# First expert table: GpSimd makes half of each low part from a copy that ScalarE takes out of PSUM, and the residual rests in DRAM meanwhile

## The chip, the cores and the metric

One core of one Trainium2 chip runs the whole program. The metric is the device time of one execution in microseconds (us). The kernel before took 3082.72 us, the median of 3 runs (3081.7 to 3082.83).

## What is computed

The program is a layer of a language model on 512 tokens of width 1024, followed by two more blocks (attention, gated linear attention, feed-forward). The change lies in the first layer's mixture of experts, which has 16384 experts of one row each in two tables, `u_tab` and `v_tab`:

```python
def block_fn(xb):
    T = xb.shape[0]
    q = (xb @ wq).reshape(T, PEER_HEADS, 2, PEER_KHALF)
    s = jnp.einsum('thpc,hpnc->thpn', q, keys)
    v1, i1 = lax.top_k(s[:, :, 0], PEER_TOPK)
    v2, i2 = lax.top_k(s[:, :, 1], PEER_TOPK)
    ...
    sc, pos = lax.top_k(cand, PEER_TOPK)
    idx = jnp.take_along_axis(cidx, pos, axis=-1)
    gate = jax.nn.softmax(sc, axis=-1)
    ug = jnp.take(u_tab, idx, axis=0)
    act = jax.nn.gelu(jnp.einsum('td,thkd->thk', xb, ug), approximate=False)
    vg = jnp.take(v_tab, idx, axis=0)
    return jnp.einsum('thk,thkd->td', gate * act, vg)
```

There are 8 heads with 16 chosen experts each, so 128 experts per token. The result is added to the residual `x`. All of it is float32.

## The kernel before, in words

**Stages.** `peer_scores` (from about 450 us) makes the queries and their scores against the keys. `first_choice_and_memory` chooses the experts of the first 128 tokens. `experts_first` (about 600 to 1302 us) goes through the first table, `experts_second` (to about 1840 us) through the second. Between these functions all engines meet at the end of a block. In `peer_scores` SyncE loads the key tiles (L2163) and query weights (L250) in turn; in `experts_second` GpSimd gathers rows of v (L3147) as it gathered rows of u, and SyncE begins the loads of the next stage's weights (L448) when the last tile has been used.

**float32 in three passes.** A float32 factor is split into a high part, which TensorE multiplies at full rate, and a low part, the exact value minus the high one. A product is then three matmuls: high by high, low by high, high by low (`three_passes`, L207 to L209).

**`experts_first` (L2721).** The table has 128 tiles of 128 experts. The first 128 tokens are done exactly by gathering the rows they chose; the other 384 are multiplied with every expert, and the unwanted results get a gate of zero later. For each tile b:

- SyncE loads 128 raw rows of u, 512 KB, into one of two buffers (L2644).
- TensorE turns them (eight transposes of 128x128, L3012) into two PSUM banks, `ps_u[0]` and `ps_u[1]`, four transposes each. It is three tiles ahead: it turns tile b+3 before it multiplies tile b. Half n of a turn waits until VectorE has read that bank.
- ScalarE copies both banks as the high half (L2940, two instructions of 128x512). VectorE makes the low half (`make_low`, L2846): PSUM minus high, two instructions of 128x512. The high and low parts lie in four slots.
- TensorE multiplies: 24 matmuls of 384 columns. ScalarE applies Gelu (L2950) and stores the result (L2952).
- GpSimd gathers, for the routed tokens, one row of u per token (an indirect DMA, `fetch`, L2823) into one of four row buffers, and VectorE takes the dot product of each row with its token (L2851). `fetch(b+1)` waits until `dot(b-3)` has freed its buffer. `take_list` (L2815) gives it the next four columns of the list of experts.

**What else runs in the stage.** For each of the three remaining groups of 128 tokens there is a choice phase of 24 tiles and a gate phase of 16 tiles. In the choice phase VectorE runs the top-16 search in 24 chunks, one between every two tiles (`topk.numbers`, with lines such as L2315, L2320, L2375, L2378). In the gate phase it builds float16 marks of the chosen experts (`build`, L2896 to L2900), TensorE sums them into gates (`sum_gates`, L3034), ScalarE takes these out of PSUM (L2961) and stores 1 MB for every 32 tokens (L2965). Between the two phases TensorE waits for VectorE's signal `chosen` and turns the chosen numbers and gates (L3047). Eight tiles remain at the end. A tile takes 5.04 us in the choice phase and 5.98 us in the gate phase.

**The order of the work.** Each engine's queue is in order and written out by hand; semaphores join them. VectorE's order for tile b is: a chunk of the choice (or `build`), both halves of `make_low(b+3)`, then `dot(b)`. ScalarE's is the high part of tile b+3, the Gelu of tile b, the gates. GpSimd's is `fetch(b+1)`, and a `take_list` before every fourth.

**The residual.** `c.x` holds x, 2 MB in SBUF, from the start of the layer until `experts_second` adds the experts' result to it at its end (L3247).

Of the kernel before, what the change touches and what calls it, by code (L numbers as in the profile page):

```python
# [2125 lines left out]
WQ_SLOTS = 4  # L2126


def peer_scores(nc, c, weights, late, keys_t, scores, topk, ahead):

# [7 lines left out]
    with ExitStack() as ctx:  # L2140
# [12 lines left out]
        with nc.Block() as block:  # L2153
            @block.sync
            def _(sp):
                ahead.load(sp)
                for j in range(tiles):
                    t = j + 2
                    if slots <= t < tiles:
                        weights.load(sp, t // slots, t % slots)  # L2160
                    if j >= slots:
                        sp.wait_ge(scored, j - slots + 1)
                    sp.dma_start(keys[:, j % slots, :], keys_t[j, :, :]).then_inc(loaded[j % slots], 16)  # L2163
                sp.wait_ge(weights.low_made, tiles + 2)
                ahead.load_first_keys(sp)

            @block.gpsimd
            def _(pool):
# [475 lines left out]
        sp.dma_start(self.raw[:, b % 2, :], self.tiles[bass.ds(i * BODY + b, 1), :, :].rearrange("a p d -> (a p) d")).then_inc(self.loaded[b % 2], 16)  # L2644


class SecondTable:


# [65 lines left out]
def experts_first(nc, c, u, table, act_d, g_d, topk, h_n, dots, second):  # L2715
# [18 lines left out]
    with ExitStack() as ctx:  # L2734
# [5 lines left out]

        halves = c.h[:, :, :].rearrange("p (r a) n -> p r (a n)", r=4)
        raw, loaded = table.raw, table.loaded
        high = [x[:, :, :] for x in second.high] + [c.h_high[:, :, 0:P]]
        low = [x[:, :, :] for x in second.low] + [c.h_low[:, :, 0:P]]
        rows = [topk.scores[:, 0, n * 8:(n + 1) * 8, :].rearrange("p a k -> p (a k)") for n in range(2)]
# [18 lines left out]
        u_turned = sem("u_turned")  # L2764
        high_made = sem("high_made")
        low_made = sem("low_made")
        used = sem("used")
        act_kept = sem("act_kept")
        act_stored = second.act_stored
# [17 lines left out]
        with nc.Block() as block:  # L2787
# [23 lines left out]

            @block.gpsimd
            def _(pool):
                def take_list(i, b):
                    nc.gpsimd.tensor_copy(list_[:, b % 8:b % 8 + 4], topk.idx[:, bass.ds(i * BODY + b, 4)]).then_inc(listed, 1)  # L2815
                    pool.wait_ge(listed, i * 2 + b // 4 + 1)
                    pool.sem_inc(list_seen, 1)

                def fetch(i, b):

                    pool.wait_ge(dotted, i * BODY + b + 1)
                    pool.sem_inc(row_seen, 1)
                    nc.gpsimd.indirect_dma_start(rows[b % 4], None, u,  # L2823
                                                 bass.IndirectOffsetOnAxis(ap=list_[:, b % 8:b % 8 + 1], axis=0)).then_inc(fetched[b % 4], 16)

                def tiles(i, last):
                    for b in range(BODY):
                        if b + 1 < BODY or not last:
                            if b % 4 == 3:
                                take_list(i, b + 1)  # L2830
                            fetch(i, b + 1)

                pool.iota(line_i[:, :], pattern=[[1, KEYS]], base=0, channel_multiplier=0).then_inc(line_made, 1)
                take_list(0, 0)
                fetch(0, 0)
                with pool.Fori(0, KEYS // BODY - 1) as i:
                    tiles(i, False)
                tiles(KEYS // BODY - 1, True)

            @block.vector  # L2840
            def _(dve):
                def make_low(i, b):
                    for n in range(2):
                        dve.wait_ge(high_made, i * (2 * BODY) + 2 * b + n + 1)
                        ks = slice(4 * n, 4 * n + 4)
                        nc.vector.tensor_tensor(low[b % SLOTS][:, ks, :].bitcast(F32R), ps_u[n][:, :, :], high[b % SLOTS][:, ks, :],  # L2846
                                                ALU.subtract).then_inc(low_made, 1)

                def dot(i, b):
                    dve.wait_ge(fetched[b % 4], (i * (BODY // 4) + b // 4) * 16 + 16)  # L2850
# [83 lines left out]
            def _(act):  # L2934
                def make_high(i, b):

                    act.wait_ge(used, i * BODY + b + 1)
                    for n in range(2):
                        act.wait_ge(u_turned, i * (2 * BODY) + 2 * b + n + 1 + 4)
                        nc.scalar.activation(high[b % SLOTS][:, 4 * n:4 * n + 4, :].bitcast(F32R), ps_u[n][:, :, :], ACT.Copy).then_inc(high_made, 1)  # L2940

                def tile(i, b):
                    make_high(i, b + ahead)
                    keep(i, b)
# [23 lines left out]
                act.sem_inc(act_kept, 2)  # L2968
                act.sem_inc(gates_kept, 2)
                act.sem_inc(used, SLOTS)  # L2970
                for n in range(2):
                    act.sem_inc(act_stored[n], 16)
                    act.sem_inc(gates_stored[n], 16)
# [29 lines left out]
            def _(pe):  # L3003
# [3 lines left out]

                def turn_from(rows_in, i, b):
                    for n in range(2):
                        pe.wait_ge(low_made, i * (2 * BODY) + 2 * b + n + 1)  # L3010
                        for k in range(4 * n, 4 * n + 4):
                            mm = nc.tensor.transpose(ps_u[n][:, k - 4 * n, :], rows_in[:, k * P:(k + 1) * P], c.ident[:, :])  # L3012
                        mm.then_inc(u_turned, 1)
# [3 lines left out]
                    products(i, b)  # L3017

                def products(i, b):
                    pe.wait_ge(low_made, i * (2 * BODY) + 2 * b + 2 + 2)  # L3020
                    pe.wait_ge(act_kept, i * BODY + b + 1)
                    for k in range(DT):
                        mm = three_passes(nc, ps[b % 2][:, 0:DENSE], high[b % SLOTS][:, k, :], low[b % SLOTS][:, k, :],
                                          c.h_high[:, k, P:S], c.h_low[:, k, P:S], start=(k == 0), stop=(k == DT - 1))
                    mm.then_inc(used, 1)
# [8 lines left out]
                            mm = nc.tensor.matmul(ps_g[n % 2][:, m, :], second_hot[:, slot, t, :], first[:, slot, j, t, :], start=(j == 0), stop=(j == 1))  # L3034
                    mm.then_inc(grouped, 1)

                pe.sem_inc(low_made, 2)
                for b in range(ahead):
                    pe.wait_ge(table.head_loaded[b], 16)
                    turn_from(table.head[b], 0, b)  # L3040
# [16 lines left out]
                    products(0, b)  # L3057


def experts_second(nc, c, v, act_d, second, idx, dots, gate, following, first):  # L3060

# [4 lines left out]
    with ExitStack() as ctx:  # L3068
# [33 lines left out]
        with nc.Block() as block:  # L3102
            @block.sync
            def _(sp):
                def load(i, b, last):
                    sp.wait_ge(low_made, i * (2 * BODY) + b + 1)
                    second.load(sp, i, b)
                    if last and b >= 2 * BODY - 2:
                        sp.wait_ge(second.act_stored[b % 2], (KEYS // 2) * 16 + 16)

                    sp.wait_ge(made, i * (2 * BODY) + b + 1)
                    second.load_act(sp, act_d, i, b)

                def turn(i, first, last):
                    for b in range(2 * BODY):
                        if not first or b >= 4:
                            load(i, b, last)
                        if b % oct_ == 3 and not (last and b > oct_):

                            r = b // oct_  # L3120
                            if r == 0:
                                second.load_gates(sp, i, 1)
                            else:
                                second.load_gates(sp, i + 1, 0)

                sp.sem_inc(low_made, 4)
                sp.sem_inc(made, 4)
                turn(0, True, False)
                with sp.Fori(1, KEYS // (2 * BODY) - 1) as i:
                    turn(i, False, False)  # L3130
                turn(KEYS // (2 * BODY) - 1, False, True)
                sp.wait_ge(made, KEYS + 4)
                for b in range(first):
                    following.load(sp, b)
# [57 lines left out]
            def _(dve):  # L3192
# [49 lines left out]
                turn(KEYS // per - 1, True)  # L3242
                dve.wait_ge(row_summed, KEYS + 4)
                nc.vector.tensor_tensor(row_sum[:, 0, :], row_sum[:, 0, :], row_sum[:, 1, :], ALU.add).then_inc(rows_added, 1)
                for k in range(DT):
                    dve.wait_ge(row_turned, k + 1)
                    nc.vector.tensor_tensor(c.x[:, k, :], acc[k][:, :], c.x[:, k, :], ALU.add).then_inc(added, 1)  # L3247
# [1369 lines left out]
def experts(nc, c, a, late, weights, lasting):  # L4617
# [3 lines left out]
    with ExitStack() as ctx:  # L4621
# [6 lines left out]
        dots = sb("dots", [P, HEADS * TOPK])  # L4628
        scores = sb("scores", [P, ST, 2 * HEADS, KEYS])
        second = SecondTable(nc, c, a["v"], g_d, scores)  # L4630
        with nc.sbuf_tensor("norm2_unit_high", [P, DT, S], F32, align_bytes=ALIGN) as c.h_high, \
                nc.sbuf_tensor("norm2_unit_low", [P, DT, S], F32, align_bytes=ALIGN) as c.h_low:
            with ExitStack() as inner:
                topk = TopK(nc, c, inner, scores, idx, gate)
                memory = MemoryAhead(nc, c, a)
                peer_scores(nc, c, weights, late, a["keys_t"], scores, topk, memory)
                late.room.close()
                table = FirstTable(nc, c, a["u"])
                first_choice_and_memory(nc, c, a, topk, h_n, table, memory)
                second.share(ctx, lasting)  # L4640
                experts_first(nc, c, a["u"], table, act_d, g_d, topk, h_n, dots, second)
        retire_semaphores(c)
        stream = qkv_stream(nc, c, a)
        half = DT // 2
        stream.early = {b: tuple(x[0][:, b * half:(b + 1) * half, :].rearrange("p k n -> p (k n)") for x in (second.high, second.low)) for b in range(2)}
        experts_second(nc, c, a["v"], act_d, second, idx, dots, gate[:, 0, :], stream, 4)
    return stream


# [396 lines left out]
```

## Time and profile before

| what | value |
|---|---|
| median of 3 runs | 3082.72 us (3081.7 to 3082.83) |
| profiled execution, its span | 3083.4 us |
| TensorE (PE) busy, share of the span | 3001.1 us, 97% |
| VectorE (DVE) busy | 2225.1 us, 72% |
| GpSimd (POOL) busy | 1124.6 us, 36% |
| ScalarE (ACT) busy | 981.6 us, 32% |
| DMA | 507.91 MB, mean 165 GB/s |

The span is the time between the first and the last event of one profiled execution; the runs were timed apart from it. Of the profiled execution only the span is listed, so the span serves as its own time; it is 0.7 us over the runs' median. A busy share is an average over stages that are limited by different things, so it doesn't tell what a change in one stage is worth.

### The profile page before, as it was taken

Reading aid. Unit: us, or ns where it says so; the run is one execution under the profiler, and the core shown is the slowest. Engines: PE = TensorE matmul, PEld = TensorE weight load, DVE = VectorE, ACT = ScalarE, POOL = GpSimd, SP = SyncE. Lnnn points to the kernel's source line nnn. Section 1 sums busy time; section 2 is a strip of 40 time slices with the busy share of each in tenths; the row PEclk is TensorE's granted clock in tenths of the full one; section 3 lists DMA queues with packets and bytes.
Section 4 is the critical chain, followed back from the end, with each engine's and each line's share of the span. In section 5 each row is a group of like instructions: output and inputs, shape, how many; then the busy total and the mean of one; then the engine's idle time right before and its main releaser. Section 6 shows DMA issues by size and latency. Waiting matters only on the chain. (4 is left out here: it accounts for less than half of the span.)

```text
span 3083.4 us, 55647 instructions
## 1 busy us (share of the span) xinstructions
PE 3001.1 (97%) x20151; PEld 2650.7 (86%) x20151; DVE 2225.1 (72%) x3952; ACT 981.6 (32%) x1828; POOL 1124.6 (36%) x806
## 2 busy tenths in 40 slices
PE   9999989899999999999999999999999999899999
PEld 7688868799999999999999997768888878688887
DVE  8766687798898898688888887677775345577741
ACT  3444430334433334333333333561111023321110
POOL 4234235222122222243333334214555443345553
PEclk9999999999999999999999999999999999899999
DMA  4000032377877878899999953112223241123233
GB/s 171 28 3 3 3 113 78 131 241 254 299 247 263 286 251 268 297 388 359 352 348 340 354 202 105 33 55 89 96 99 92 79 99 35 58 88 99 98 92 93
DMA packets 242033, 507.91 MB, mean 165 GB/s; under 512 B 44566, under 2 KB 135846, under 8 KB 238412
## 3 DMA queue, kind: packets, MB, share of 16 engines
q1 hardware_dynamic: 183116, 321.11, 31.0%
q0 software_dynamic: 36864, 134.23, 13.4%
q10 hardware_dynamic: 21888, 50.34, 4.2%
q8 instruction: 106, 1.74, 0.2%
q14 instruction: 59, 0.48, 0.0%
HBM read 453.17 MB, written 52.44 MB: 164 GB/s over the span
## 5 line engine op out<-in xcount | busy, mean ns | idle before, releaser
L202 POOL TENSOR_TENSOR up_low<-normed,up_high 128x1024 fp32r<-128x1024 f32 (+1 forms) x136 | 317.0, 2331 | 299.9 <-DVE up_high L197 299.9
L3147 POOL DMA_INDIRECT ev_rows<-in_v,ev_list x128 | 177.3, 1385 | 326.5 <-DVE ev_row_sum L3214 313.6
L207 PE MATMUL up_ps<-ffn_high,up_high 128*128 128x512 f32 x704 | 274.9, 390 | 3.0 <-DVEq L833 3.0
L209 PE MATMUL up_ps<-ffn_high,up_low 128*128 128x512 f32 x704 | 273.9, 389 | 0.0
L208 PE MATMUL up_ps<-ffn_low,up_high 128*128 128x512 f32 x704 | 273.9, 389 | 0.0
L207 PE MATMUL eu_ps<-norm_unit_high,expert_high 128*128 128x384 f32 x768 | 265.7, 346 | 0.0
L209 PE MATMUL eu_ps<-norm_unit_high,expert_low 128*128 128x384 f32 x768 | 258.2, 336 | 0.0
L208 PE MATMUL eu_ps<-norm_unit_low,expert_high 128*128 128x384 f32 x768 | 257.9, 336 | 0.0
L197 DVE CAST up_high<-normed 128x1024 fp32r<-128x1024 f32 (+1 forms) x136 | 92.5, 680 | 205.4 <-PE up_down_ps L209 150.6
L2823 POOL DMA_INDIRECT expert_scores<-in_u,eu_list x64 | 84.0, 1313 | 268.3 <-DVE eu_dots L2851 260.0
L3172 ACT ACTIVATE expert_high<-mixed 128x1024 fp32r<-128x1024 f32 x95 | 100.8, 1061 | 229.3 <-PE ev_acc L209 212.9
L2846 DVE TENSOR_TENSOR expert_low<-eu_turned,expert_high 128x512 fp32r<-128x512 f32 x192 | 123.8, 686 | 66.2 <-ACT expert_high L2940 65.2
L207 PE MATMUL ev_acc<-ev_w_high,expert_high 128*128 128x384 f32 x512 | 171.1, 334 | 0.0
L209 PE MATMUL ev_acc<-ev_w_high,expert_low 128*128 128x384 f32 x512 | 171.0, 334 | 0.0
L208 PE MATMUL ev_acc<-ev_w_low,expert_high 128*128 128x384 f32 x512 | 171.0, 334 | 0.0
L2950 ACT ACTIVATE mixed<-eu_ps 128x384 f32<-128x384 f32 x128 | 62.8, 491 | 329.4 <-PE eu_ps L209 329.4
L3214 DVE SCALAR_TENSOR_TENSOR ev_row_sum<-ev_rows,ev_weight,ev_row_sum 128x1024 f32<-128x1024 f32 x128 | 164.3, 1285 | 3.4 <-DMA ev_rows<-in_v,ev_list 3.4
L791 ACT ACTIVATE mixed<-up_ps,columns_sb 128x512 f32<-128x512 f32 x88 | 68.6, 779 | 297.2 <-DVE up_ps L821 297.2
L2823 POOL DMA_INDIRECT normed<-in_u,eu_list x64 | 68.7, 1073 | 256.5 <-DVE eu_dots L2851 255.8
L3207 DVE TENSOR_TENSOR expert_low<-mixed,expert_high 128x1024 fp32r<-128x1024 f32 x95 | 117.9, 1241 | 60.4 <-ACT expert_high L3172 60.4
L207 PEld LDWEIGHTS up_ps<-ffn_high,up_high 128*128 128x128 f32 x704 | 132.1, 188 | 31.5 <-DVEq L833 3.8
L208 PEld LDWEIGHTS up_ps<-ffn_low,up_high 128*128 128x128 f32 x704 | 132.1, 188 | 27.7 <-issue 0.5
(721 smaller groups left out, 8633.5 us busy)
## 6 DMA issues: line engine op xcount, KB each, us to landing
mixed<-in_v SPq DMA_DIRECT2D x128, 512.0 KB
normed<-in_u SPq DMA_DIRECT2D x125, 512.0 KB
normed<-in_w_up SPq DMA_DIRECT2D x88, 512.0 KB, 3.4
expert_act<-mixed ACTq DMA_DIRECT2D x128, 192.0 KB
expert_gates<-eu_gates ACTq DMA_DIRECT2D x24, 1024.0 KB
expert_scores<-expert_gates SPq DMA_DIRECT2D x16, 1536.0 KB
normed<-expert_act SPq DMA_DIRECT2D x128, 192.0 KB
normed<-in_w_down SPq DMA_DIRECT2D x32, 448.0 KB, 3.3
```

Source lines behind the costliest of these rows:

```text
L197: return nc.vector.tensor_copy(high.bitcast(F32R), of)
L202: return nc.gpsimd.tensor_tensor(low.bitcast(F32R), of, high, ALU.subtract)
L207: nc.tensor.matmul(out, w_high.bitcast(F32R), x_high.bitcast(F32R), start=start, stop=False)
L208: nc.tensor.matmul(out, w_high.bitcast(F32R), x_low.bitcast(F32R), start=False, stop=False)
L209: return nc.tensor.matmul(out, w_low.bitcast(F32R), x_high.bitcast(F32R), start=False, stop=stop)
L791: nc.scalar.activation(cv[:, s, :], ps[s][:, :], ACT.Identity, scale=c.cols[:, bass.ds(j + at + 2 * 2 * FT, 1)], bias=c.cols[:, bass.ds(j ...
L2823: nc.gpsimd.indirect_dma_start(rows[b % 4], None, u, bass.IndirectOffsetOnAxis(ap=list_[:, b % 8:b % 8 + 1], axis=0)).then_inc(fetched[b % ...
L2846: nc.vector.tensor_tensor(low[b % SLOTS][:, ks, :].bitcast(F32R), ps_u[n][:, :, :], high[b % SLOTS][:, ks, :], ALU.subtract).then_inc(low_ ...
L3147: nc.gpsimd.indirect_dma_start(rows[:, b % 4, :], None, v, bass.IndirectOffsetOnAxis(ap=list_[:, b % 8:b % 8 + 1], axis=0)).then_inc(fetch ...
L3172: nc.scalar.activation(high[b % SLOTS][:, :, :].bitcast(F32R), raw[:, b % 4, :, :], ACT.Copy).then_inc(high_made, 1)
L3207: nc.vector.tensor_tensor(low[b % SLOTS][:, :, :].bitcast(F32R), raw[:, b % 4, :, :], high[b % SLOTS][:, :, :], ALU.subtract).then_inc(low ...
L3214: nc.vector.scalar_tensor_tensor(out=row_sum[:, b % 2, :], in0=rows[:, b % 4, :], scalar=weight[:, bass.ds(i * per + b, 1)], in1=row_sum[: ...
```

## The change

In `experts_first`, VectorE makes only the first half of each tile's low part. For the second half ScalarE copies bank `ps_u[1]` a second time, as it is, into one of two SBUF buffers (`copied`, the first two 128x512 pieces of `c.x`), and GpSimd subtracts the high part from that copy. TensorE's second half turn now waits for ScalarE's copy instead of VectorE's second half, and its products wait for both low halves. ScalarE's copy of tile b waits until GpSimd has read the copy of tile b-2 (`copy_low_made`). In GpSimd's loop the new `make_low(b+3)` stands ahead of `fetch(b+1)`, and the first three low parts stand ahead of the `iota`, the first list and the first fetch.

Since `c.x` is used as a buffer, the residual is stored to DRAM by SyncE in `peer_scores`, and loaded back by SyncE at the end of `experts_second`, where VectorE waits for it before its last addition. The program also clears its semaphores once more ahead of `experts_first`: `TopK` and `FirstTable` are created before `peer_scores` with their semaphores kept apart, and GpSimd clears the retired ones at the start of the block.

```diff
 def peer_scores(...):
                 ahead.load(sp)
+                residual.store(sp)
                 for j in range(tiles):
...
                 ahead.load_first_keys(sp)
+                sp.wait_ge(residual.stored, 16)
...
+class ResidualAway:
+    def __init__(self, nc, c):
+        self.x, self.away = c.x, nc.dram_tensor("residual_away", [P, DT, S], F32).ap()
...
+    def store(self, sp):
+        sp.dma_start(self.away, self.x[:, :, :]).then_inc(self.stored, 16)
+    def load(self, sp):
+        sp.dma_start(self.x[:, :, :], self.away).then_inc(self.loaded, 16)
...
 def experts_first(...):
+        copied = c.x[:, 0:2, :]
...
             @block.gpsimd
             def _(pool):
+                clear_stale(nc, c)
...
+                def make_low(i, b):
+                    pool.wait_ge(copy_made, i * BODY + b + 1 + 1)
+                    pool.sem_inc(copy_met, 1)
+                    take_low(nc, low[b % SLOTS][:, 4:8, :], copied[:, b % 2, :].rearrange("p (k n) -> p k n", n=P), high[b % SLOTS][:, 4:8, :]).then_inc(copy_low_made, 1)
+
                 def tiles(i, last):
                     for b in range(BODY):
+                        if b + ahead < BODY or not last:
+                            make_low(i, b + ahead)
                         if b + 1 < BODY or not last:
                             if b % 4 == 3:
                                 take_list(i, b + 1)
                             fetch(i, b + 1)
 
+                for b in range(ahead):
+                    make_low(0, b)
                 pool.iota(...)
...
             @block.vector
             def _(dve):
                 def make_low(i, b):
-                    for n in range(2):
-                        dve.wait_ge(high_made, i * (2 * BODY) + 2 * b + n + 1)
-                        ks = slice(4 * n, 4 * n + 4)
-                        nc.vector.tensor_tensor(low[b % SLOTS][:, ks, :].bitcast(F32R), ps_u[n][:, :, :], high[b % SLOTS][:, ks, :],
-                                                ALU.subtract).then_inc(low_made, 1)
+                    dve.wait_ge(high_made, i * (2 * BODY) + 2 * b + 1)
+                    nc.vector.tensor_tensor(low[b % SLOTS][:, 0:4, :].bitcast(F32R), ps_u[0][:, :, :], high[b % SLOTS][:, 0:4, :],
+                                            ALU.subtract).then_inc(low_made, 1)
...
             def _(act):
...
+                    act.wait_ge(copy_low_made, i * BODY + b + 1)
+                    nc.scalar.activation(copied[:, b % 2, :].rearrange("p (k n) -> p k n", n=P), ps_u[1][:, :, :], ACT.Copy).then_inc(copy_made, 1)
...
             def _(pe):
...
-                        pe.wait_ge(low_made, i * (2 * BODY) + 2 * b + n + 1)
+                        pe.wait_ge(copy_made if n else low_made, i * BODY + b + 1)
...
                 def products(i, b):
-                    pe.wait_ge(low_made, i * (2 * BODY) + 2 * b + 2 + 2)
+                    pe.wait_ge(low_made, i * BODY + b + 1 + 1)
+                    pe.wait_ge(copy_low_made, i * BODY + b + 1 + 2)
                     pe.wait_ge(act_kept, i * BODY + b + 1)
...
 def experts_second(...):
                 turn(KEYS // (2 * BODY) - 1, False, True)
+                residual.load(sp)
                 sp.wait_ge(made, KEYS + 4)
...
+                dve.wait_ge(residual.loaded, 16)
                 for k in range(DT):
                     dve.wait_ge(row_turned, k + 1)
                     nc.vector.tensor_tensor(c.x[:, k, :], acc[k][:, :], c.x[:, k, :], ALU.add).then_inc(added, 1)
...
             with ExitStack() as inner:
+                taken, c.taken = c.taken, []
                 topk = TopK(nc, c, inner, scores, idx, gate)
+                table = FirstTable(nc, c, a["u"])
+                c.apart, c.taken = c.taken, taken
...
-                table = FirstTable(nc, c, a["u"])
                 first_choice_and_memory(nc, c, a, topk, h_n, table, memory)
                 second.share(ctx, lasting)
+                retire_semaphores(c)
                 experts_first(...)
```

## Rows read from the trace of the kernel before

A row of windows gives the busy time and, in brackets, the instructions of PE, PEld, DVE, ACT and POOL in this order. Rows of a timeline give start and length in us.

**Rows 1.** Windows: stretch, length, busy us (count) by engine, clock, DMA share, GB/s.

```profile
843.00:957.00 114.00, 113.16 (x733) 112.16 (x731) 101.99 (x270) 39.35 (x74) 28.76 (x28) 1.00 0.74 245
957.00:1053.00 96.00, 96.00 (x761) 93.61 (x760) 79.06 (x145) 41.45 (x81) 21.49 (x21) 1.00 0.86 289
600.00:1302.00 702.00, 697.12 (x4870) 684.64 (x4868) 587.84 (x1363) 267.97 (x498) 160.99 (x159) 0.99 0.79 266
```

**Rows 2.** Waits of PE, 610 to 1300 us: total us, times, longest us.

```profile
PE eu_g L3034 <- DVE eu_first L2900: 2.5, 3, 0.9
```

**Rows 3.** Timeline, 683 to 692 us: start, length, engine, line, operation, count, [idle before].

```profile
685.13 1.03 PE L3012 MATMUL eu_turned<-ident,normed 128*128 128x128 f32 x8
...
686.40 0.10 DVE L2320 MATCH_VALUE_LOAD topk_pos<-topk_top,mixed 128x8 f32 x1
...
686.53 1.09 ACT L2940 ACTIVATE expert_high<-eu_turned 128x512 fp32r<-128x512 f32 x2 [0.62 <-PE eu_turned L3012]
...
689.56 1.28 DVE L2846 TENSOR_TENSOR expert_low<-eu_turned,expert_high 128x512 fp32r<-128x512 f32 x2
...
690.31 1.25 PE L3012 MATMUL eu_turned<-ident,normed 128*128 128x128 f32 x8
```

**Rows 4.** Lines by form, GpSimd: busy us, mean ns, idle us before.

```profile
L202 POOL TENSOR_TENSOR norm_unit_low<-normed,norm_unit_high 128x512 fp32r<-128x512 f32 x8 | 10.3, 1287 | 9.5 <-DVE norm_unit_high L197 9.5
```

**Rows 5.** Timeline of GpSimd and VectorE, 2143 to 2149 us.

```profile
2144.50 2.39 POOL L202 TENSOR_TENSOR up_low<-normed,up_high 128x1024 fp32r<-128x1024 f32 x1 [2.60 <-DVE up_high L197]
...
2144.84 2.60 DVE L809 TENSOR_TENSOR mixed<-mixed 128x512 f32<-128x512 f32 x1
...
2147.58 0.43 DVE L197 CAST ff_high<-mixed 128x512 f32 x1
...
2148.61 1.30 POOL L202 TENSOR_TENSOR ff_low<-mixed,ff_high 128x512 f32 x1 [1.72 <-DVE ff_high L197]
```

**Rows 6.** Timeline of GpSimd, 596 to 616 us.

```profile
601.52 0.94 POOL L2823 DMA_INDIRECT expert_scores<-in_u,eu_list  x1 [0.30 <-issue]
```

**Rows 7.** Timeline of VectorE and GpSimd, 700 to 712 us.

```profile
710.93 2.29 DVE L2375 TENSOR_TENSOR mixed<-topk_part_f,topk_ranks 128x2048 f32<-128x2048 f32 x1
...
711.82 2.21 POOL L2823 DMA_INDIRECT normed<-in_u,eu_list  x1 [3.73 <-DVE eu_dots L2851]
```

**Rows 8.** Source L3147, the second table's gathers: issue to landing.

```profile
DMA to landing us min/median/max: 4.5/7.5/10.0
```

**Rows 9.** Timeline, 957 to 970 us, the gate phase.

```profile
962.12 1.04 PE L3012 MATMUL eu_turned<-ident,normed 128*128 128x128 f32 x8
...
963.32 1.29 DVE L2900 TENSOR_TENSOR eu_first<-eu_marks,eu_part 128x1024 f16<-128x1024 f16 x2
...
964.24 1.09 ACT L2940 ACTIVATE expert_high<-eu_turned 128x512 fp32r<-128x512 f32 x2 [0.62 <-ACT eu_gates L2961]
...
967.19 1.07 PE L3034 MATMUL eu_g<-eu_first,eu_second 128*128 128x128 f16 x16
...
968.10 1.04 PE L3012 MATMUL eu_turned<-ident,normed 128*128 128x128 f32 x8
```

**Rows 10.** Timeline of PE, 724 to 746 us.

```profile
730.87 0.38 PE L3047 MATMUL eu_sel_ps<-ident,topk_number 128*128 128x128 f32 x2
```

**Rows 11.** Source L127, the clearing of semaphores: ns min, median, max.

```profile
L127 POOLq EVENT_SEMAPHORE_RANGE_CLEAR  x12: 46/157/640, 390.1 to 2643.6; - x12
```

**Rows 12.** Windows 460 to 464 us; timeline of SyncE's queue, 455 to 475 us.

```profile
460.00:462.00 2.00, 2.00 (x10) 1.61 (x10) 0.54 (x1) 1.32 (x2) 1.90 (x1) 1.00 0.90 342
462.00:464.00 2.00, 2.00 (x11) 1.65 (x10) 1.90 (x4) 0.00 (x0) 0.51 (x1) 1.00 0.19 50
...
471.83 0.33 SPq L2163 DMA_DIRECT2D wq_keys<-in_keys_t  x1
```

**Rows 13.** Timeline of SyncE's queue and VectorE, 1800 to 1834 us.

```profile
1819.56 1.75 SPq L448 DMA_DIRECT2D normed<-in_w_qk  x4
...
1833.48 0.69 DVE L3247 TENSOR_TENSOR residual<-ev_acc,residual 128x512 f32<-128x512 f32 x1 [3.41 <-PE ev_acc L3260]
```

More of the change, by code:

```diff
@@ L2126, with peer_scores @@
 WQ_SLOTS = 4
-def peer_scores(nc, c, weights, late, keys_t, scores, topk, ahead):
+def peer_scores(nc, c, weights, late, keys_t, scores, topk, ahead, residual):
     slots = WQ_SLOTS
@@ L2644, in load @@
         sp.dma_start(self.raw[:, b % 2, :], self.tiles[bass.ds(i * BODY + b, 1), :, :].rearrange("a p d -> (a p) d")).then_inc(self.loaded[b % 2], 16)
+class ResidualAway:
+    def __init__(self, nc, c):
+        self.x, self.away = c.x, nc.dram_tensor("residual_away", [P, DT, S], F32).ap()
+        self.stored, self.loaded = nc.alloc_semaphore(name="residual_stored"), nc.alloc_semaphore(name="residual_loaded")
+    def store(self, sp):
+        sp.dma_start(self.away, self.x[:, :, :]).then_inc(self.stored, 16)
+    def load(self, sp):
+        sp.dma_start(self.x[:, :, :], self.away).then_inc(self.loaded, 16)
 class SecondTable:
@@ L2766, in experts_first @@
         low_made = sem("low_made")
+        copy_made = sem("copy_made")
+        copy_low_made = sem("copy_low_made")
+        copy_met = sem("copy_met")
         used = sem("used")
@@ L2970, in _ @@
                 act.sem_inc(used, SLOTS)
+                act.sem_inc(copy_low_made, 2)
                 for n in range(2):
@@ L3035, in sum_gates @@
                     mm.then_inc(grouped, 1)
-                pe.sem_inc(low_made, 2)
+                pe.sem_inc(low_made, 1)
+                pe.sem_inc(copy_made, 1)
                 for b in range(ahead):
@@ L3057, in _, with experts_second @@
                     products(0, b)
-def experts_second(nc, c, v, act_d, second, idx, dots, gate, following, first):
+def experts_second(nc, c, v, act_d, second, idx, dots, gate, following, first, residual):
     ahead = SLOTS - 1
@@ L4630, in experts @@
         second = SecondTable(nc, c, a["v"], g_d, scores)
+        residual = ResidualAway(nc, c)
         with nc.sbuf_tensor("norm2_unit_high", [P, DT, S], F32, align_bytes=ALIGN) as c.h_high, \
@@ L4633, in experts @@
             with ExitStack() as inner:
+                taken, c.taken = c.taken, []
                 topk = TopK(nc, c, inner, scores, idx, gate)
+                table = FirstTable(nc, c, a["u"])
+                c.apart, c.taken = c.taken, taken
                 memory = MemoryAhead(nc, c, a)
-                peer_scores(nc, c, weights, late, a["keys_t"], scores, topk, memory)
+                peer_scores(nc, c, weights, late, a["keys_t"], scores, topk, memory, residual)
                 late.room.close()
-                table = FirstTable(nc, c, a["u"])
                 first_choice_and_memory(nc, c, a, topk, h_n, table, memory)
                 second.share(ctx, lasting)
+                retire_semaphores(c)
                 experts_first(nc, c, a["u"], table, act_d, g_d, topk, h_n, dots, second)
@@ L4645, in experts @@
         stream.early = {b: tuple(x[0][:, b * half:(b + 1) * half, :].rearrange("p k n -> p (k n)") for x in (second.high, second.low)) for b in range(2)}
-        experts_second(nc, c, a["v"], act_d, second, idx, dots, gate[:, 0, :], stream, 4)
+        experts_second(nc, c, a["v"], act_d, second, idx, dots, gate[:, 0, :], stream, 4, residual)
     return stream
```

## The prediction, written before the changed kernel was run

> **What bounds the kernel now.** I first cut the span into stretches to see which engine fills the one that the change is in. From 600 to 1302 us (the first expert table) TensorE is busy 697.1 of 702 us at a granted clock of 0.99; in the stretch beside the choice of experts 113.2 of 114 us, in the one with the gates 96.0 of 96.0 [rows 1]. VectorE has 102.0 of 114 us, so it is nearly full too, ScalarE and GpSimd are not. Then I asked what TensorE waits for: from 610 us on, three waits of 0.8 us each, for the first marks of each gate phase [rows 2]. So VectorE's subtraction is beside a full TensorE: all that TensorE idles here is 702 - 697.1 = 4.9 us, and that is the most that any relief can give in this stage, 0.16% of the kernel. The timeline of a tile [rows 3] shows the one place where VectorE is late with the low part: after eight searches (686.40 to 689.56) its subtraction ends half a tile at 690.16, and the next turn starts at 690.31, 0.14 us after the 5.04 us that a tile takes. About 0.4 us in all; it happens in the first table alone.
>
> **The change, part by part.** Measured chances: about 0.2% (6 us) is what can be told from no change.
>
> 1. Engines' sums. VectorE loses one 0.69 us subtraction per tile (two in 1.28, a pitch of 0.60 [rows 3]): 128 x 0.60 = 77 us. ScalarE gains one copy at its pitch, 1.09 - 0.60 = 0.49 [rows 3]: 63 us on 268. GpSimd gains 128 subtractions of 1.29 us [rows 4] = 165 us on 161. None of these reaches TensorE's 697, so by sums nothing changes; gain at most the 0.4 us above. ScalarE's new wait, ahead of its copy, is for GpSimd's low part of two tiles before; the Gelu and the gates stand behind it, but that part is made some 6 us earlier by the loop below: 0, and if GpSimd should fall a whole tile behind, it is the loop that shows it. TensorE's new wait before its products is for a low part made three tiles ahead: 0.
>
> 2. A wait put before the gathers. This is the term that decides. GpSimd's queue is in order. Before, it waits only for a free row buffer, four deep, and the row for tile b is asked for three tiles early. Now it does low(b+3), which waits for the copy of tile b+3, and only then fetch(b+1). So the gather of row b can't start until low(b+2) is made, and behind that gather stands VectorE's dot(b), behind that one chunk of the choice and the first half of low(b+4), and TensorE's turn(b+5) waits for that half. That closes a loop over three tiles. Its room is 3 x 5.04 = 15.12 us. Its length, counted from the start of turn(b+2): second copy ended 2.49 (685.13 to 687.62) and the new one 0.49 more, 2.98 [rows 3]; GpSimd's wake after a semaphore, 0.60 in one place [rows 5], between that and nothing: 0.3; low 1.29 [rows 4]; 0.30 to the next GpSimd instruction [rows 6]; gather G; dot 1.15 (its 1.22 overlaps); chunk C; half a low 0.60; TensorE's wake 0.15 [rows 3]. In sum 6.8 + G + C, so G + C may be 8.35.
>
> C from the code's 24 chunks a table: three of 3.16 us (eight searches or replacements, [rows 3]), two of 2.6, seven of 2.3 (2048 wide [rows 7]), the others 2.1 or less, 2.15 in the mean. G, from issue to landing, isn't printed for this table; the same gather of the second table takes 4.5 us at the least, 7.5 in the middle, 10.0 at the most [rows 8], there with DMA nearly full, here with a share of 0.74 to 0.86 [rows 1]. Ends 4.5 and 7.5; I take 6.0, half-way, because the share lies between a free and a full one.
>
> With G = 6.0, C over 2.35 stalls TensorE: three times 0.8, twice 0.27, and the five two-input 2048-wide chunks if something adds 0.65. It does: GpSimd's issue of a gather took 2.21 us instead of 0.94 beside such an operation [rows 7], 1.27 more; half of it, since it has to meet. That is 2.4 + 0.5 + 3.0 = 6 us a table. A stall lengthens the room of the next two tiles, and the heavy chunks follow each other, so I count half: 3 a table, 9 us. The Trainium skill (page SBUF — State Buffer, section Who interferes with whom) infers that a tensor_tensor with two SBUF inputs takes only the read interface that it shares with GpSimd, and so leaves the writing of descriptors free. Here the trace disagrees, by the 2.21 us; by the page the 3.0 would be gone, and this term 4.5 us instead of 9.
>
> 3. The same loop in the gate phase. Room 3 x 5.98 = 17.94 for the turn (962.12, 968.10), but the marks of tile b+1 are wanted earlier, at 2 x 5.98 + 5.07 = 17.03 (967.19) [rows 9]. Length: copy ended 3.21 + 0.49 = 3.70 [rows 9]; wake 0.3; low 1.29 plus a lock wait of 0.35 (half of one f16 operation); 0.30; gather 6.3 (its issue is 0.27 longer here); dot 1.15: 13.4. Then four f16 operations, 2.5 (two in 1.29 [rows 9]), one held by GpSimd's low for 0.65: that GpSimd's subtraction blocks a two-input operation is shown by one of 2.60 us, begun under a GpSimd subtraction of 2.39 [rows 5]; half of 1.29 is taken. 16.5 against 17.03. It holds in the mean and not where the 1 MB gate writes meet the gather: 1 us a table, 3 us.
>
> 4. Changes of phase. dot(22) of a table comes at turn(24) + 11.4 from part 2's sum (2.98 + 0.3 + 1.29 + 0.30 + 6.0, with 0.5 of waiting), then 2.3 and 0.9 for the gates, then the signal that TensorE waits for at 730.87 [rows 10]; turn(24) is three tiles before, 715.75: 715.75 + 11.4 + 1.15 + 3.2 = 731.5. 0.6 us late, three times: 2 us. Before, it was there in time.
>
> 5. The start: GpSimd now makes three low parts before its first gather, so dot(0) moves back by some 4 us, which VectorE has caught up but for 0.5 us when turn(7) wants low(6). The clear of stale semaphores costs at most 0.64 us a piece [rows 11] before the first copy exists: 0. At the end the last three gathers come together: 0 to 1 us, 0.5.
>
> 6. The residual. SP's store of 2 MB stands ahead of four key loads and two weight loads. The queues move 342 GB/s until the loads end at 462, as the DMA share's fall to 0.19 shows; 2.1 MB at that rate take 6 us, so these land at 468, and the first score ends at 471.8, where SP's next key load is let go [rows 12]. Cover 3.8 us: 0; without it, up to 6. The load back is issued after the last tile's loads, ahead of the next weight loads at 1819.56; VectorE idles 3.41 us before it adds onto the residual [rows 13], which hides a last gather that is late: 0; without that cover 3.
>
> Sum: 9 + 3 + 2 + 1 - 0.4, about +14. The profiled execution has a span of 3083.4, 0.7 over the median of 3082.7, so 3097 by its own time, 3096 as a median.
>
> **The rivals.** (a) The gather lands in time. G = 4.5: G + C stays under 8.35 in every chunk, the gate phase has 2 us of room, and only a lock here or there is left: 3083, from 3079 to 3089. For it speaks that the loop's mean, 6.8 + 6.0 + 2.15 = 14.95, is still under 15.12, and that fewer row transfers are now in flight at once. It decides at G = 5.2, where the heaviest chunk just fits. (b) The gather binds in every tile, G = 7.5: 16.45 against 15.12, 1.3 in three tiles, 0.44 x 72 = 32 us, the gate phase some 6 more: 3121. Against it speaks the DMA share. (c) TensorE wins back what it idles: 4.9 us, 3078; the start's share of that can't go, and this would still be no change by 0.2%. To be faster than that something outside the stage must shrink, and nothing there is touched.
>
> **How the numbers follow.** Forecast, some tiles stall: 3096, from 3089 to 3112, chance 0.48. (a) 0.37, of which a tenth above 3089. (b) 0.10. (c) and what I don't see 0.05. Range 3080 to 3121: its lower end is (a)'s, the upper (b)'s. Slower by over 0.2%: 0.48 + 0.10 + 0.02 = 0.60; within: 0.36; faster: 0.04.
>
> **What would show it.** Right: waits of TensorE's turn for VectorE's low part in the choice phases, above all at the searches 256 wide; VectorE waiting for the gather before its dot product, which it never does before; fetches one tile before their dot instead of three; a tile of 5.04 us stretched to 5.5 here and there. Wrong: no VectorE wait for the gather (G short), or one in each tile (b); any change in the stages of the residual's transfers.

## The result, and the profile after

The changed kernel took 3147.17 us (median of 4 runs, 3132.61 to 3152.59) against 3082.21 us for the kernel before: a ratio of 1.0207, 95% interval 1.0183 to 1.0231, some 65 us slower. The direction was forecast; the size was not, and it lies above the upper end of the range (3121). Measured again, the same kernel took 3136.8 us against 3082.17 and, on another chip, 3135.9 against 3081.91, so 54 to 65 us is the effect. (One slip in the description of the kernel: a 1 MB store of gates covers 16 tokens, not 32; there are 24 of them.)

The profiled execution has a span of 3143.2 us, 59.8 over the one of before. The stretch of 600 to 1302 us, read as in [rows 1], shows TensorE no longer full, and its clock lower:

```profile
600.00:1302.00 702.00, 655.23 (x4468) 637.61 (x4467) 515.82 (x1184) 306.04 (x577) 328.57 (x268) 0.97 0.72 239
```

655.2 us busy instead of 697.1, VectorE 515.8 instead of 587.8: both wait. What TensorE waits for from 600 to 1380 us, as in [rows 2] (total us, times, longest):

```profile
PE eu_g L3069 <- DVE eu_first L2930: 19.6, 10, 3.5
PE eu_turned L3046 <- DVE expert_low L2876: 16.3, 15, 2.6
PE eu_turned L3046 <- DVE norm_unit_low L2876: 12.8, 9, 2.4
```

That is 48.7 us in 34 waits, 29.1 of them for VectorE's half low part and 19.6 for the gate marks. The waits of VectorE in the same stretch name what is behind it:

```profile
DVE normed L2881 <- DMA normed<-in_u,eu_list: 110.3, 37, 5.6
DVE expert_scores L2881 <- DMA expert_scores<-in_u,eu_list: 66.9, 26, 5.6
```

177.2 us in 63 waits for gathered rows, which it never waited for before. One turn of the loop that the prediction describes stands in the timeline of 903 to 930 us:

```profile
903.42 1.09 PE L3046 MATMUL eu_turned<-ident,normed 128*128 128x128 f32 x8 [0.63 <-DVE expert_low L2876]
...
905.08 0.61 ACT L2973 ACTIVATE residual<-eu_turned 128x512 f32<-128x512 f32 x1
...
905.87 2.19 POOL L202 TENSOR_TENSOR expert_low<-residual,expert_high 128x512 fp32r<-128x512 f32 x1 [2.70 <-ACT residual L2973]
...
908.22 1.76 POOL L2845 DMA_INDIRECT normed<-in_u,eu_list  x1 [0.15 <-issue]
...
916.09 1.22 DVE L2881 CUSTOM_DVE_ANT_0 normed<-normed,expert_h_n 128x1024 f32<-128x1024 f32 x1 [3.72 <-DMA normed<-in_u,eu_list]
```

Turn of tile 53 at 903.42, ScalarE's copy to 905.69, GpSimd's low part to 908.06, the gather of row 51 from 908.22, VectorE idle 3.72 us until it starts its dot product at 916.09. Then come eight searches, the half low part of tile 55 (920.40 to 921.07), and only then the turn of tile 56, at 921.13: 17.71 us for three tiles that had room for 15.12. What TensorE does next is in the windows of that place (after the five busy times stand the granted clock, the DMA share and GB/s):

```profile
920.00:921.00 1.00, 0.00 (x0) 0.00 (x0) 1.00 (x4) 0.00 (x0) 0.00 (x0) 1.00 0.78 135
921.00:922.00 1.00, 0.87 (x9) 0.87 (x9) 0.73 (x2) 0.17 (x1) 0.00 (x0) 1.00 0.92 299
922.00:923.00 1.00, 1.00 (x7) 1.00 (x5) 1.00 (x6) 1.00 (x3) 0.00 (x0) 0.61 0.84 324
923.00:924.00 1.00, 1.00 (x5) 1.00 (x4) 1.00 (x5) 0.40 (x1) 0.42 (x1) 0.50 0.62 131
...
925.00:926.00 1.00, 1.00 (x6) 1.00 (x5) 1.00 (x4) 0.00 (x0) 0.95 (x1) 0.69 0.10 37
926.00:927.00 1.00, 1.00 (x8) 1.00 (x7) 1.00 (x2) 0.00 (x0) 0.00 (x0) 1.00 0.33 57
```

It had idled 2.35 us; from 922.2 to 925.6 its clock is 0.50 (1.2 GHz), and the tile takes 6.66 us though it waits for nothing. The whole account of the 59.8 us: from 610 us to the last tile the gaps between TensorE's instructions of over 0.25 us are 47.3 us in 32 places (before: 2.5 in 3), and seven stretches at 0.50 of the clock, 27.3 us together, cost half of that, 13.7 us, if TensorE would have been busy all through them (before: none, but for one at the start of the stage, which both kernels have). 44.8 + 13.7 = 58.5 of 59.8, as an estimate. Counted by tiles (without the first tile of the stage), the choice phases take 39.6 us more than 5.04 us a tile (before: 1.4), the gate phases 27.0 more than 5.98 (before: 2.9).

### The profile page after: what moved, and what is told of

Its sections match the earlier page's. It is cut to its first block and busy times, and to the rows that moved or that the text cites. A ratio compares the mean times of both kernels' runs of the same rounds, so it can differ in the third digit from the quotient of the medians.

```text
span 3143.2 us, 55796 instructions
## 1 busy us (share of the span) xinstructions
PE 3018.5 (96%) x20151; PEld 2659.4 (85%) x20151; DVE 2185.1 (70%) x3824; ACT 1045.5 (33%) x1956; POOL 1326.9 (42%) x934
## 5 line engine op out<-in xcount | busy, mean ns | idle before, releaser
L202 POOL TENSOR_TENSOR expert_low<-residual,expert_high 128x512 fp32r<-128x512 f32 x96 | 143.4, 1494 | 290.1 <-ACT residual L2973 287.3
L2881 DVE CUSTOM_DVE_ANT_0 normed<-normed,expert_h_n 128x1024 f32<-128x1024 f32 x64 | 87.5, 1368 | 110.4 <-DMA normed<-in_u,eu_list 110.3
L3046 PE MATMUL eu_turned<-ident,normed 128*128 128x128 f32 x1000 | 135.9, 280 | 28.4 <-DVE expert_low L2876 15.6
```

What stands on the lines that cost most here:

```text
L202: return nc.gpsimd.tensor_tensor(low.bitcast(F32R), of, high, ALU.subtract)
L2881: nc.vector.tensor_tensor_reduce(out=rows[b % 4], in0=rows[b % 4], in1=h_n[:, :], scale=1.0, scalar=0.0, op0=ALU.mult, op1=ALU.add, accum_ ...
```

## The experiments

Theory L is the loop of waits. Theory P: GpSimd's subtraction slows VectorE and the gathers by itself, whatever its place. Theory R: the residual's transfers or the clearing of semaphores cost the time.

**order1: the fetch ahead of the low part.**

```diff
                     for b in range(BODY):
-                        if b + ahead < BODY or not last:
-                            make_low(i, b + ahead)
                         if b + 1 < BODY or not last:
                             ...
                             fetch(i, b + 1)
+                        if b + ahead < BODY or not last:
+                            make_low(i, b + ahead)
```

> Theory L (a loop of waits): with the low part ahead of the fetch in GpSimd's queue, turn(b+2), ScalarE's copy, GpSimd's low part, the gather of row b, its dot product, a chunk of the choice, half a low part and turn(b+5) form a loop that the changed kernel's trace shows 15.2 us long against the 15.12 us of three tiles. Here fetch(b+1) is issued ahead of low(b+3), so row b only waits for low(b+1), and the loop goes over four tiles, 20.16 us. L expects that VectorE's 177 us of waiting for gathered rows go to under 20 us, that the tile is 5.04 us nearly everywhere, and about 3083 us (3079 to 3090). Theory P (GpSimd's subtraction itself slows VectorE and the gathers, whatever its order): the time stays, 3132 to 3152 us.

Measured: 3082.87 us against 3082.38, ratio 1.000 (0.9991 to 1.001). The two instructions of GpSimd's queue, in the other order, give back all that the change lost. VectorE's waits for rows, in the same view as above:

```profile
DVE expert_scores L2881 <- DMA expert_scores<-in_u,eu_list: 9.6, 6, 3.3
DVE normed L2881 <- DMA normed<-in_u,eu_list: 0.8, 2, 0.7
```

10.4 us instead of 177.2. P falls here, and more than that: the marks of the gate phase collide with GpSimd's subtraction more in order1 than in the changed kernel, and the loss is gone all the same. The line of the marks, by lines, in order1 first and in the changed kernel in the second fence (busy us, mean ns):

```profile
L2926 DVE TENSOR_TENSOR eu_marks<-eu_line,eu_key 128x1024 f16<-128x1024 bf16 x48 | 71.6, 1492 | 3.7 <-PE eu_g L3069 2.3 <-DVE eu_part L2907 1.3
```

```profile
L2926 DVE TENSOR_TENSOR eu_marks<-eu_line,eu_key 128x1024 f16<-128x1024 bf16 x48 | 43.6, 908 | 3.7 <-DVE expert_dots L2886 2.3 <-DVE eu_part L2907 1.3
```

What P leaves in order1 is one small wait of TensorE, for the first marks of each gate phase:

```profile
PE eu_g L3069 <- DVE eu_first L2930: 4.4, 3, 1.5
```

It was 2.5 us before [rows 2]. At each of the three changes of phase the first marks operation takes 1.31 to 1.33 us instead of 0.69, and TensorE waits 1.48 us instead of 0.84: 1.9 us in all.

**residual_only: all but the half low part** (VectorE makes both halves again; store, load and clearing stay).

```diff
-                    dve.wait_ge(high_made, i * (2 * BODY) + 2 * b + 1)
-                    nc.vector.tensor_tensor(low[...][:, 0:4, :], ps_u[0], high[...][:, 0:4, :], ...)
+                    for n in range(2):
+                        dve.wait_ge(high_made, i * (2 * BODY) + 2 * b + n + 1)
+                        nc.vector.tensor_tensor(low[...][:, ks, :], ps_u[n], high[...][:, ks, :], ...)
...
-                    nc.scalar.activation(copied[...], ps_u[1][:, :, :], ACT.Copy).then_inc(copy_made, 1)
...
-                            make_low(i, b + ahead)
```

> Everything of the change but the half low part: the residual goes to DRAM and back, the semaphores are cleared once more, VectorE makes both halves as before. L and P: no change, 3082 us within 3. Theory R (the transfers or the clearing cost the time): over 3110 us.

Measured: 3081.77 us, ratio 0.9995 (0.9986 to 1.0005). R falls.

**copy2 and copy3: ScalarE takes the copy twice, or three times** (copy2 without the second of the added lines).

```diff
                     act.wait_ge(copy_low_made, i * BODY + b + 1)
+                    nc.scalar.activation(c.x[:, 2 + b % 2, :]..., ps_u[1][:, :, :], ACT.Copy)
+                    nc.scalar.activation(c.x[:, 4 + b % 2, :]..., ps_u[1][:, :, :], ACT.Copy)
                     nc.scalar.activation(copied[:, b % 2, :]..., ps_u[1][:, :, :], ACT.Copy).then_inc(copy_made, 1)
```

> ScalarE takes the copy twice, the first time into a part of the residual's place that nothing reads, so copy_made comes 0.6 us later. ScalarE was busy 306 of 702 us and has room. L: the loop gets 0.6 us longer over three tiles, 0.2 us a tile at the most: 112 x 0.2 = 22 us, half of it where there is slack: 11 to 22 us more, about 3163 us. P: no change, about 3147 us.

Measured: 3142.09 us (3139.99 to 3149.64), a miss: under the first 3147.17, and 6 us over the 3135.90 that the changed kernel took on the same chip at another time. Without the changed kernel measured beside it, it settles nothing; so a larger dose follows, beside the changed kernel.

> The changed kernel once more, on the same chip and beside the same runs of the kernel before as the three that follow, because copy2 came out at 3142.1 us and its runs and those of the changed kernel (3132.6 to 3152.6 us) overlap. L: a loop that sits at its room amplifies every difference of the gathers, so 3130 to 3155 us, and its own profile gives the baseline for the others.

> ScalarE takes the copy three times, the first two into parts of the residual's place that nothing reads, so copy_made comes some 1.0 to 1.2 us later than in the changed kernel. L: 15 to 40 us above after_again (at the most 1.2 / 3 x 112 = 45). P, or any theory in which the delay between copy and gather doesn't count: as after_again.

Measured: after_again 3136.80 us (3134.91 to 3138.84), copy3 3164.06 (3158.35 to 3178.18): 27.3 us more. By the timelines of the two, the copy ends 0.96 us later after the start of its turn; so a microsecond of delay costs some 28 us in the whole, though ScalarE is busy only 414.7 of 702 us:

```profile
600.00:1302.00 702.00, 647.96 (x4375) 626.19 (x4374) 507.65 (x1172) 414.67 (x801) 312.98 (x263) 0.97 0.69 235
```

Where it is lost wasn't foreseen. Counted by tiles as above, the gate phases lose 27.0, 27.5 and 21.5 us in the three profiles of the changed kernel, 34.5 in copy2's and 41.5 in copy3's. The choice phases don't follow the dose: 39.6, 32.7 and 33.3 us in the changed kernel, 24.7 in copy2, 34.8 in copy3. In these counts the stretches at half the clock are in, 13.7 us in copy3 against 5.1 in after_again. Why the choice phases don't follow stays open.

**lists: only take_list moved ahead of the low part.**

```diff
+                        if b % 4 == 3 and (b + 1 < BODY or not last):
+                            take_list(i, b + 1)
                         if b + ahead < BODY or not last:
                             make_low(i, b + ahead)
                         if b + 1 < BODY or not last:
-                            if b % 4 == 3:
-                                take_list(i, b + 1)
                             fetch(i, b + 1)
```

> Only take_list is moved ahead of the low part; the fetch stays behind it. L: in the changed kernel the gap between the low part and the fetch is 1.03 us before every fourth gather and 0.15 us before the others; the 0.88 us leaves the loop for 32 rows, some of which wait for slack anyway, so 8 to 20 us come back, about 3133 us. P: no change, 3132 to 3152 about 3147 us.

Measured: 3133.20 us (3130.07 to 3134.18), without the changed kernel beside it; so once more.

> The changed kernel beside the two that follow, on the same chip: 3130 to 3155 us.

> lists came out at 3133.2 us on another chip than the changed kernel's 3147.2 and 3136.8, so it is measured again beside the changed kernel. From copy3 (27 us for 1.0 to 1.2 us more in the loop) the loop gives some 25 us for each microsecond; take_list is 0.88 us on every fourth row, 0.22 us in the mean, so L expects 5 us less than after_third, up to 14 (what the first two runs differ by). P: none.

Measured: after_third 3135.90 us (3133.80 to 3141.22), lists_again 3122.28 (3118.25 to 3126.82). 13.6 us come back beside it, 2.7 by the first measurement. But the two measurements of this one kernel, on one chip, lie 10.9 us apart with ranges that don't touch, so the times alone don't show that the step is on the path. The profiles speak for it: the choice phases lose 23.2 us in lists and 17.5 in lists_again, against 32.7 to 39.6 in the changed kernel, the gate phases about as much as there (27.0 and 28.9). Its size is known to some 10 us only. In the profile of the changed kernel this step is one row of GpSimd's waits:

```profile
POOL expert_scores L2845 <- POOL eu_list L2837: 28.1, 31, 0.9
```

0.9 us, 31 times, that the sum of the prediction didn't have.

**wait_only: the wait without the work.** From residual_only, GpSimd waits for the high part and does nothing with it.

```diff
+                def meet(i, b):
+                    pool.wait_ge(high_made, i * (2 * BODY) + 2 * b + 2)
+                    pool.sem_inc(high_met, 1)
...
                     for b in range(BODY):
+                        if b + ahead < BODY or not last:
+                            meet(i, b + ahead)
                         if b + 1 < BODY or not last:
```

> From residual_only (VectorE makes both halves, no copy, no subtraction on GpSimd), GpSimd only waits, ahead of fetch(b+1), until ScalarE has made the high part of tile b+3: the wait alone. L: the loop is the changed kernel's less the copy (0.49 us) and the low part (1.47), some 13.3 us against 15.12, so that only gathers of over 7 us, about one in eight, stall TensorE, by a microsecond or so: 3090 us (3084 to 3100), and VectorE waits for rows where it never did before. P: no work was added, so 3082.

Measured: 3095.75 us (3094.29 to 3101.94) against 3082.17, ratio 1.0053 (1.0037 to 1.0068). A wait alone, with no work behind it, costs 13.6 us. VectorE and TensorE wait:

```profile
DVE expert_scores L2878 <- DMA expert_scores<-in_u,eu_list: 43.6, 19, 5.6
DVE normed L2878 <- DMA normed<-in_u,eu_list: 34.4, 22, 4.7
```

```profile
PE eu_turned L3039 <- DVE expert_low L2873: 7.4, 5, 2.8
...
PE eu_turned L3039 <- DVE norm_unit_low L2873: 1.7, 3, 0.6
```

Its tiles lose 11.1 us in the choice phases (12.5 against 1.4) and nothing in the gate phases (2.9, as before). Its two longest choice tiles, 7.99 and 7.69 us instead of 5.04, each stand behind a single gather of 9.4 us, for which VectorE waited 5.65 and 5.41 us.

**low_beside: the wait and a subtraction of the same size.** To wait_only's `meet` is added, on parts of the residual's place:

```diff
+                    take_low(nc, c.x[:, 2, :], c.x[:, 0, :], c.x[:, 1, :]).then_inc(beside_made, 1)
```

> wait_only with a subtraction of 128x512 on GpSimd between the wait and the fetch, on parts of the residual's place that nothing else reads; VectorE still makes both halves, ScalarE takes no copy. L: the loop is wait_only's with 1.29 + 0.15 us more, and the changed kernel's with the copy's 0.49 us less; between 3095.8 and 3136.8 us, which are 1.96 us of the loop apart, that is 3095.8 + 1.44 / 1.96 x 41 = 3126 us (3112 to 3140). If the subtraction counted only by holding up VectorE's two-input operations, VectorE would show it in its operations' lengths and not in waits for rows. If the wait alone were the matter: 3096.

Measured: 3121.87 us (3116.78 to 3126.21) against 3081.91. Against the kernel before it is 40.0 us, the wait alone 13.6, the changed kernel beside it 54.0: the wait, 26 us for the subtraction, 14 for the copy and the rest. wait_only ran on another chip, so these steps are rough. VectorE's relief is missing here, and yet most of the loss is there, so the loss doesn't come from the relief.

**order3: the gathers as early as before.** Three rows are fetched at the start, and fetch(b+3) stands behind low(b+3), two tiles earlier than the changed kernel's fetch(b+1) (the expectation says three).

```diff
                             make_low(i, b + ahead)
-                        if b + 1 < BODY or not last:
-                            if b % 4 == 3:
-                                take_list(i, b + 1)
-                            fetch(i, b + 1)
+                            if b % 4 == 1:
+                                take_list(i, b + 3)
+                            fetch(i, b + 3)
...
-                fetch(0, 0)
+                for b in range(3):
+                    fetch(0, b)
```

> The change with the gathers three tiles earlier: the first three rows are fetched at the start, and behind low(b+3) stands fetch(b+3), so the loop goes over five tiles, 25 us. L: as order1 or a little under it, since no row can be late any more: 3081 us (3078 to 3085); VectorE's waits for rows go to nothing. P: 3132 to 3152.

Measured: 3085.23 us against 3082.17, ratio 1.0013 (1.0004 to 1.0022): as L says in the main, but not under order1, and just over the expected range. In its profile 1.9 us more than before are lost at the first marks of the gate phases, as in order1, and 1.7 more in the choice phases; why was not followed up. No version was found that beats the kernel before; TensorE's idle time there allowed 4.9 us at most.

## Why the prediction was wrong

**Right: what bounds, the mechanism, the place.** VectorE's relief gave TensorE nothing; GpSimd's low part ahead of the fetch closes the loop over three tiles; its marks in the profile are the ones named (TensorE's turn waiting for the half low part, VectorE for rows, fetches one tile before their dot product). order1 takes the loop away and, but for the 1.9 us above, all of the loss with it. The residual (part 6) costs nothing, as said (residual_only is at 0.9995), and the start (0.5 us in part 5) nothing either: the first turns of the stage begin 2.0 us earlier than before.

**The loop's parts were nearly right.** Over the 71 choice tiles of the changed kernel: copy ended at 2.89 us (said: 2.98), wake 0.20 (0.3), low part 1.47 (1.29), to the fetch 0.40 (0.30), dot and chunk 3.81 (3.30), half low 0.68 (0.60), turn 0.06 where it was held back (0.15). 9.51 against the 8.92 of part 2's sum with its 2.15 for the chunk. The gather, by the source view of its line:

```profile
DMA to landing us min/median/max: 4.0/5.8/10.9
```

I had taken 6.0, between the ends 4.5 and 7.5 of [rows 8]. The low part is longer than in [rows 4]:

```profile
L202 POOL TENSOR_TENSOR expert_low<-residual,expert_high 128x512 fp32r<-128x512 f32 x96 | 143.4, 1494 | 290.1 <-ACT residual L2973 287.3 <-DVE eu_dots L2881 2.7
```

In the timeline of 903 to 930 us one takes 2.19 us that begins under a two-input operation of VectorE (904.62 to 906.91), and the next 1.29. With the 5.64 us that the gathers of these 71 tiles take in the mean, the loop is 15.15 us long against its room of 15.12; I had 14.95. Missing were take_list (0.9 us before one fetch in four) and 0.5 us in dot and chunk.

**The step that failed: "I count half: 3 a table, 9 us", with one gather time for all rows.** Part 2 let only the chunk vary, found which chunks exceed 2.35 us, and halved that. But the gathers spread from 4.0 to 10.9 us, and a loop near its room pays for a late row and gets nothing for an early one, since no choice tile takes less than its 5.04 us. The changed kernel's trace shows it row by row: in 18 of the 71 choice tiles the loop held TensorE's turn back by more than 0.25 us, 24.9 us together, and before each VectorE had waited 1.3 to 4.8 us for a row. The gathers of these 18 took 6.92 us in the mean, those of the other 53 took 5.21; dot and chunk, which part 2 let vary, were alike (3.85 and 3.80). wait_only shows it too: its loop is some 13.3 us long in the mean, 1.8 under the room; by part 2's method it would cost nothing, and it cost 13.6 us. The choice phases lost 38.2 us (39.6 - 1.4) where part 2 said 9.

**Changes of phase: 6.7 us instead of part 4's 2.** At the first one two tiles took 10.45 and 7.89 us instead of 6.98 and 5.96; VectorE waited 4.45 us for a row there. The other two took 7.60 instead of 6.96: part 4's 0.6 us each, but not for its reason. TensorE doesn't wait there for `chosen`; it waits 1.48 us instead of 0.84 for the first marks, as in order1, where hardly a row is late. That these two came out in size was luck.

**The gate phase: 24.1 us (27.0 - 2.9), of which 6.7 are the changes of phase; the other 17.4 instead of 3.** Part 3 had "it holds in the mean and not where the 1 MB gate writes meet the gather: 1 us a table". The mean does hold: the row lands 11.5 us after its turn starts, where I had 12.2. But the rows are not alike: of the gathers of a gate phase every fourth takes 7.7 us in the mean (6.3 to 8.6), the other three 5.1 to 5.9. Past the changes of phase TensorE waits for marks seven times, and each time behind one of these fourth rows. Gathers begun 2 to 6 us after a gate store take 7.2 us in the mean, those begun 6 to 14 us after it 5.4. That the store is the cause is argued from this order in time and wasn't tried by itself; two in four begin in its shadow and only one of them is that long (7.7 us against 6.4), which speaks for something besides. So why the fourth row is late stays open.

**Not in the sum at all: TensorE's clock.** The prediction priced a stall at its length. After seven stretches of waiting TensorE ran at 0.50 of its clock (1.2 GHz) for a while, which is 13.7 us of the losses above. The Trainium skill has the rule (page TensorE: Matmul & The Clock Gate, section Part 1: The HAM clock gate): the gate falls to half rate after idleness. The trace agrees in that each low stretch begins in a gap of 2.1 to 3.6 us or within 1.1 us of its end, but other gaps of 2.35, 2.71 and 2.79 us are followed by none. So its price is not fixed: after_again waited as much (47.7 us in 32 places) and lost 5.1 us by the clock.

**The rivals.** (b), the gather binding in each tile, with 38 us and 3121, was nearest in size, for another reason than its own: not longer gathers, but uneven ones. (a) had for it that the loop's mean is under its room; wait_only shows that this is not enough.

**VectorE and GpSimd beside each other.** Of the 4.5 us that hung on the Trainium skill's inference in part 2 nothing can be told in so large an effect. The Trainium skill (page SBUF — State Buffer, section Who interferes with whom) also has the rule that a VectorE instruction with two SBUF inputs contends with a GpSimd instruction that reads SBUF, and one with at most one SBUF input doesn't. This is borne out in order1: the marks, two SBUF inputs, 1492 ns instead of 689, and VectorE's half low part, which reads PSUM and one SBUF operand, 689 as against 686. The gather's instruction reads its list of rows (`eu_list`) from SBUF, so the 2.21 us of [rows 7] may be this rule, and do not refute the inference as part 2 says.

## What to carry to other kernels

An instruction added to an in-order queue delays what stands behind it by its wait as well as by its length (13.6 us for the wait alone, some 26 more for the subtraction): before adding one, ask what the next instruction of that queue was early for, and put it behind that (here the order of two lines is worth 54 us). Price a prefetch that becomes shallow by the spread of its latencies, not by their mean, as a loop near its room pays for late ones and is paid for none; and add what TensorE's clock takes after a stall.

## What the runs showed that was not expected

- Relief moved to GpSimd need not arrive. In order1 VectorE does 128 subtractions less (77 us), and is busy 590.0 of 702 us against 587.8 before: the marks take 38.5 us more (71.6 against 33.1), the dot products 15.9 (171.5 against 155.6), four of the choice's operations 10.8, the small copies of finished dot products (L2886) 12.8: 78 of the 79 that bring the sum up again.
- GpSimd's issue of a gather was 1.76 us instead of 0.94 beside a dot product, which was itself 1.59 us instead of 1.22 (908.22 and 907.55 in the timeline of the changed kernel): both are stretched where they meet.
- A loop at its room is noisy: the changed kernel's runs spread over 20 us (3132.61 to 3152.59), though only over 4 and 7 in after_again and after_third; copy3's over 20 too, those of the kernel before and of order1 over some 4 to 10.
